# State-space layer: octets 0 and 1 driven between projection chunks 4 and 5, multiplier powers and later weights behind them on VectorE

## What is computed

```
u = h @ w_in                                   # 256 x 1024
lam_bar = exp(lam * dt)                        # 64 groups x 64 states, complex
b_bar = ((lam_bar - 1) / lam) * b
x[t] = lam_bar * x[t-1] + b_bar @ u[t]
y = real(c @ x) + d_skip * u
g = gelu(y)
val, gate = split(g @ w_glu)                   # 1024 -> 2 x 1024
mix = val * sigmoid(gate)
```

## Time and profile before

| what | us |
|---|---|
| median of 3 runs (802.72 to 804.08) | 803.85 |
| span of the profiled execution | 800.8 |
| state-space stage, to the end of y(3) | 124.5 |
| first scan starts on VectorE | 64.40 |
| GLU starts on TensorE | 98.22 |

### The profile page before, as it was taken

The page is one execution under the profiler, slowest core; times in us unless marked ns, Lnnn a source line. Parts: engine busy times, 40 slices in busy tenths (PEclk is TensorE's granted clock), DMA queues, the critical chain, the costliest instruction groups (busy, mean ns, idle before and its releaser), DMA issues.

```text
span 800.8 us, 16313 instructions
## 1 busy us (share of the span) xinstructions
PE 692.0 (86%) x6452; PEld 414.8 (52%) x6452; DVE 307.7 (38%) x853; ACT 243.7 (30%) x581; POOL 49.1 (6%) x48
## 2 busy tenths in 40 slices
PE   4999699999986686585899998899999999994995
PEld 4889445556544244244344444555555555652562
DVE  6968991144110010010241633736333443331334
ACT  6672802362110010110321314435223332231224
POOL 3695000000000000000000000000000000000000
PEclk9996899999998888988999999999999999998998
DMA  9530807977999999999992465038999942999981
GB/s 244 202 110 2 227 2 290 422 299 280 422 419 421 419 421 421 420 421 417 380 387 80 170 245 215 1 115 315 416 420 421 420 206 75 423 419 421 422 341 54
DMA packets 61071, 236.35 MB, mean 295 GB/s; under 512 B 21120, under 2 KB 21328, under 8 KB 36432
## 3 DMA queue, kind: packets, MB, share of 16 engines
q1 hardware_dynamic: 60112, 235.24, 74.2%
q10 hardware_dynamic: 896, 0.24, 0.1%
HBM read 234.42 MB, written 1.05 MB: 294 GB/s over the span
## 4 chain that ended last, share of the span: by engine, by line
PE 55%; SPq 16%; DMA 12%; DVE 10%; ACT 4%; issue 2%; DVEq 0%; ACTq 0%
SPq L425 13%; PE ps L1848 11%; PE ps L1939 10%; PE ps L1765 7%; PE ps L1903 6%; PE ps L1828 5%; DMA ring<-in_moe_w_up 4%; PE ps L1868 4%; DMA hT<-in_moe_w_up 3%; DMA ring<-in_moe_w_down 3%; SPq L423 3%; PE ps L2002 2%; PE ps L2013 2%; PE ps L1911 1%; PE ps L1636 1%
## 5 line engine op out<-in xcount | busy, mean ns | idle before, releaser
L1848 PE MATMUL ps<-ring,work 128*32 128x256 f32 x1504 | 124.3, 409 | 33.2 <-DMA ring<-in_moe_w_gate 11.7
L1848 PE MATMUL ps<-work 128*32 128x256 f32 x864 | 90.8, 409 | 23.9 <-DMA ring<-in_moe_w_up 7.8
L1848 PEld LDWEIGHTS ps<-ring,work 128*32 128x32 f32 x1504 | 70.3, 118 | 73.1 <-issue 51.8
L1381 DVE TENSOR_TENSOR work<-ps,work 128x256 f32<-128x256 f32 x21 | 12.9, 613 | 190.8 <-PE ps L1848 190.8
L1848 PEld LDWEIGHTS ps<-work 128*32 128x32 f32 x864 | 50.2, 118 | 54.4 <-issue 37.9
L1903 PE MATMUL ps<-ring,work 128*32 128x512 f32 x464 | 70.7, 611 | 6.2 <-issue 5.5
L1828 PE MATMUL ps<-work,xr 128*128 128x128 bf16 x736 | 66.5, 219 | 0.7 <-DVE work L1290 0.6
L1828 PE MATMUL ps<-work 128*128 128x128 bf16 x368 | 63.9, 219 | 0.0
L1828 PEld LDWEIGHTS ps<-work,xr 128*128 128x128 bf16 x736 | 57.6, 98 | 8.9 <-issue 3.3
L1939 PE MATMUL ps<-ring,hT 128*128 128x512 f32 x128 | 56.7, 595 | 1.2 <-ACT hT L632 1.2
L1765 PE MATMUL ps<-ring,work 128*128 128x512 f32 x128 | 55.7, 593 | 0.4 <-ACT work L749 0.4
(11 more groups left out here) (337 smaller groups left out, 1115.8 us busy)
## 6 DMA issues: line engine op xcount, KB each, us to landing
ring<-in_moe_w_down SPq DMA_DIRECT2D x22, 2048.0 KB, 24.4
ring<-in_moe_w_gate SPq DMA_DIRECT2D x21, 2048.0 KB, 20.0
ring<-in_moe_w_up SPq DMA_DIRECT2D x16, 2048.0 KB, 30.6
work<-in_moe_w_up SPq DMA_DIRECT2D x12, 2048.0 KB, 20.6
work<-in_moe_w_gate SPq DMA_DIRECT2D x9, 2048.0 KB, 29.0
work<-in_moe_w_down SPq DMA_DIRECT2D x8, 2048.0 KB, 23.7
ring<-in_ssm_w_glu SPq DMA_DIRECT2D x4, 2048.0 KB, 8.7
ring<-in_attn_w_qkv SPq DMA_DIRECT2D x4, 2048.0 KB, 27.9
```

The source lines that it names most:

```text
L1848: ins = mm(ps[s, 6 + j // 2, 0:256], xg[:, k, s], pairs[slots[e // 2]][e % 2][:, k, :], start=(k == 0), stop=(k == KD - 1))
```

## The change

Input weights are written by one instruction over both groups instead of two half-height ones, so W1 has each block twice; ScalarE keeps the transposed tile with a 0/1 scale per partition (new constants C_HALF), which takes the unwanted half to zero. So W1 needs no clearing and the power-0 copy comes from Bb itself. Mu and the skip product move behind weights(2) and weights(3). VectorE stacks half of octet 1's inputs, not octet 3's. Drive(0) and drive(1) both write banks 0 and 1 and come one after the other ahead of chunk 5; the first bank of each is copied to X by ScalarE, the second by VectorE. The scratch of the scan moves out of hT, which chunks 5 to 7 still read; the carries now wait for chunk 7 (u_done 8). ScalarE's BB copies, own(0) and own(1), VectorE's second skips, and glu(2) change places.

```
-        scanP, scanQ = (hT[:, 4 * n:4 * n + 4, :].rearrange("p k t -> p (k t)") for n in range(2))
+        scanP, scanQ = pre[:, 10240:10752], pre[:, 10752:11264]
+        V_AT = (0, 0, 0, 2)
...
-            clear(first_of[:, 0:2048], 2)
-            clear(second_of[:, 0:2048], 2)
...
+                for g in range(2):
+                    act.activation(W1T[o % 2][:, i, :, 64 * g:64 * g + 64], src[:, :, g, :], ACT.Copy,
+                                   scale=con[:, C_HALF + g:C_HALF + g + 1]).then_inc(w1T_ready, 1)
...
+            stack_by(0, range(6))
             first(0)
             first(1)
+            stack_by(0, range(6, 16))
             keep_w1T(0, 0)
-            stack_by(1, range(16))
+            stack_by(1, range(8, 12))
             keep_w1T(0, 1)
+            stack_by(1, range(12, 16))
+            keep_w1T(1, 0)
             first(2)
             keep_w1T(1, 1)
             first(3)
+            keep_x(0, (0,))
+            keep_x(1, (0,))
+            act.wait_ge(cleared, 3)
...
+            stack_by(2, range(4))
             keep_w1T(2, 0)
+            stack_by(2, range(4, 16))
             keep_w1T(2, 1)
+            stack_by(3, range(4))
             keep_w1T(3, 0)
+            stack_by(3, range(4, 16))
             keep_w1T(3, 1)
-            keep_x(2)
-            keep_x(3)
+            keep_x(2, (0, 1))
             own(0)
-            own(1)
+            keep_x(3, (0, 1))
...
             keep_g(1)
+            own(1)
...
-            link(dve.tensor_copy(mu[:, 0:2, 0, :], Pw[:, 0:2, 4, :]))
-            powers(mu, 1, 1, 0, 0)
-            powers(mu, 2, 2, 1, 0)
-            powers(mu, 4, 4, 3, 0)
-            link(TS(mu[:, 2, :, :], mu[:, 1, :, :], -1.0, None, ALU.mult))
             dve.sem_inc(pow_ready, 1)
...
-                    for g in range(2):
-                        h = slice(64 * g, 64 * g + 64)
-                        ins = TTo(W1[o % 2][h, i, :, 1:4, 16 * g:16 * g + 16], v3(t1)[h], v3(second_ps)[h],
-                                  ALU.add if i else ALU.subtract)
+                    link(TTo(W1[o % 2][:, i, :, 1:4, :].rearrange("p r j (g c) -> p r j g c", g=2), spread(v3(t1), 3, 2),
+                             spread(v3(second_ps), 3, 2), ALU.add if i else ALU.subtract))
+                    dve.sem_inc(w1_ready, 1)
...
             weights(0)
             weights(1)
+            dve.wait_ge(u_done, 4)
+            for n in range(8):
+                stack(dve.tensor_copy, 1, n).then_inc(u4_late, 1)
             weights(2)
+            link(dve.tensor_copy(mu[:, 0:2, 0, :], Pw[:, 0:2, 4, :]))
+            powers(mu, 1, 1, 0, 0)
+            powers(mu, 2, 2, 1, 0)
+            powers(mu, 4, 4, 3, 0)
+            link(TS(mu[:, 2, :, :], mu[:, 1, :, :], -1.0, None, ALU.mult))
             weights(3)
+            TTo(skip, spread(con[:, C_SKIP:C_SKIP + PC], 1, KD), spread(dcol, 2, PC), ALU.mult)
             for o in range(2):
-                for b in range(2):
-                    dve.wait_ge(v_done, 2 * o + b + 1)
-                    link(inputs_kept(dve.tensor_copy, o, b))
-                    dve.sem_inc(v_kept_x, 1)
+                dve.wait_ge(v_done, 2 * o + 2)
+                link(inputs_kept(dve.tensor_copy, o, 1))
+                dve.sem_inc(v_kept_x, 1)
...
                     skips(0)
+                    dve.wait_ge(u_done, 8)
                 carries(half)
+                carried(2 * half)
+                carried(2 * half + 1)
                 if half == 0:
                     skips(1)
...
+                    if r % 4 == 0:
+                        b = r // 4
+                        pe.wait_ge(u4_ready, (16 if b == 0 else 24, 24, 40, 56)[o])
+                        if o == 1 or (o == 0 and b == 1):
+                            pe.wait_ge(u4_late, 8)
+                        if o in (1, 2):
+                            pe.wait_ge(v_kept_x if b else v_kept_late, o)
...
+            inputs(1)
+            inputs(2)
             turn_w1(0, 0)
-            inputs(5)
+            inputs(3)
             turn_w1(0, 1)
-            inputs(6)
+            inputs(4, range(4))
             turn_w1(1, 0)
-            inputs(7)
+            inputs(4, range(4, KD))
             turn_w1(1, 1)
             drive(0)
+            drive(1)
+            inputs(5)
             turn_w1(2, 0)
+            inputs(6)
             turn_w1(2, 1)
-            drive(1)
+            taps(0)
+            taps(1)
+            inputs(7)
             turn_w1(3, 0)
             drive(2)
             turn_w1(3, 1)
-            taps(0)
-            taps(1)
             drive(3)
...
             glu(0, range(4))
+            glu(2, range(4))
             pe.wait_ge(f_ready, 32)
             glu(1, range(4))
-            glu(2, range(4))
```

More of the change, by code:

```diff
@@ L67 @@
 C_TURN = C_UPTO + 9 * 8
-C_N = C_TURN + 1
+C_HALF = C_TURN + 1
+C_N = C_HALF + 2
 def slot_plan():
@@ L660, in _ @@
                 act.copy(Cc[:, i, :, :].rearrange("p r c -> p (r c)"), ps[:, 4 + i, :]).then_inc(c_ready, 1)
-            act.wait_ge(cleared, 2)
+            act.wait_ge(cleared, 1)
             for i in range(2):
@@ L671, in stack_by @@
                     stack(act.copy, b, n).then_inc(u4_ready, 1)
[L673 to L677, removed]
-                for g in range(2):
-                    h = slice(64 * g, 64 * g + 64)
-                    act.copy(BB[i][h, :, 16 * g:16 * g + 16], Bb[h, i, :, :]).then_inc(block_b, 1)
             def first(o):
@@ L686, in first @@
                 if o == 0:
-                    act.wait_ge(block_b, 4)
+                    act.wait_ge(bbar_ready, 1)
                 for i in range(2):
-                    act.copy(W1[o % 2][:, i, :, 0, :], BB[i][:, OCT * o:OCT * o + OCT, :]).then_inc(w1_first, 1)
+                    act.copy(W1[o % 2][:, i, :, 0, :].rearrange("p r (g c) -> p r g c", g=2),
+                             spread(Bb[:, i, OCT * o:OCT * o + OCT, :], 2, 2)).then_inc(w1_first, 1)
             def keep_w1T(o, i):
@@ L695, in keep_w1T, with keep_x @@
                     act.wait_ge(v_done, 2 * o - 2)
-                for b in range(2):
[L697 to L702, removed]
+                src = ps[:, 4:6, :].rearrange("p b (r g c) -> p (b r) g c", g=2, c=64)
+                for g in range(2):
+                    act.activation(W1T[o % 2][:, i, :, 64 * g:64 * g + 64], src[:, :, g, :], ACT.Copy,
+                                   scale=con[:, C_HALF + g:C_HALF + g + 1]).then_inc(w1T_ready, 1)
+            def keep_x(o, bs):
+                for b in bs:
                     act.wait_ge(v_done, 2 * o + b + 1)
@@ L709, in own @@
                 if half == 0:
-                    act.wait_ge(cleared, 6)
+                    act.wait_ge(cleared, 4)
                 for j in range(SB):
@@ L715, in own @@
                         act.copy(dst[:, :, r, 32 * (3 - j):P], kps[:, :, 0:32 * (j + 1)]).then_inc(f_ready, 1)
+            act.wait_ge(normed, 2)
+            stack_by(0, range(6))
             first(0)
             first(1)
+            stack_by(0, range(6, 16))
             keep_w1T(0, 0)
-            stack_by(1, range(16))
+            stack_by(1, range(8, 12))
             keep_w1T(0, 1)
+            stack_by(1, range(12, 16))
+            keep_w1T(1, 0)
             first(2)
-            keep_w1T(1, 0)
-            stack_by(2, range(16))
             keep_w1T(1, 1)
             first(3)
-            stack_by(3, range(8, 16))
+            keep_x(0, (0,))
+            keep_x(1, (0,))
+            act.wait_ge(cleared, 3)
+            for i in range(2):
+                for g in range(2):
+                    h = slice(64 * g, 64 * g + 64)
+                    act.copy(BB[i][h, :, 16 * g:16 * g + 16], Bb[h, i, :, :]).then_inc(block_b, 1)
+            stack_by(2, range(4))
             keep_w1T(2, 0)
+            stack_by(2, range(4, 16))
             keep_w1T(2, 1)
+            stack_by(3, range(4))
             keep_w1T(3, 0)
+            stack_by(3, range(4, 16))
             keep_w1T(3, 1)
-            keep_x(2)
-            keep_x(3)
+            keep_x(2, (0, 1))
             own(0)
-            own(1)
+            keep_x(3, (0, 1))
             def gelu(o):
@@ L1169, in local_states @@
                 tmp = [v[:, 0:256].rearrange("p (i r h) -> p i r h", i=2, r=16) for v in (scanP, scanQ)]
-                if half:
-                    dve.wait_ge(v_kept_late, 4)
+                dve.wait_ge(v_kept_late, 6 if half else 2)
                 for l in range(1, SEG):
@@ L1625, in _, with inputs @@
             turn()
-            def inputs(c):
-                if c % 4 == 0:
+            def inputs(c, ks=range(KD)):
+                if c % 4 == 0 and ks[0] == 0:
                     pe.wait_ge(landed[c // 4], 16)
@@ L1632, in inputs @@
                     pe.wait_ge(bbar_ready, 1)
-                for k in range(KD):
+                for k in ks:
                     if c == 0 and k % 2 == 0:
@@ L1637, in inputs @@
```

(14 more changed lines are left out.)

37 lines of the change are left out of this document (8 added, 29 removed).

## The result

The changed kernel takes 812.16 us (median of 4 runs, 811.12 to 813.24) against 803.97 (4 runs, 802.72 to 804.27): ratio 1.0115, 95% interval 1.0102 to 1.0127. It is slower, by 8.2 us. The profiled execution took 811.12 with a span of 809.3.

The account below looks back on a forecast made before the run. The state-space stage of 125 us, with a fixed DMA-busy tail behind it, sets the time. The GLU starts at 106.0 against 98.22, taken as +8 on span 800.8: 808.8, plus 3.05 around it, 812; range 806 to 818.

Parts of the forecast that it names:

- VectorE's front: VectorE's input weights: paired writes at 0.95 for 1.13 us, 4.06 us an octet for 4.6, weights(2) ending at 42.4.
- the walk: The prediction's step-by-step timing of the engines through the state-space stage, putting the GLU's start at 106.0 against 98.22.
- TensorE up to drive(1): TensorE's chunks, transposes and drive(0): drive(0) runs to 43.8 us, the first bank of drive(1) to 45.6.
- The wait: Drive(1)'s second bank waits for VectorE's copy behind weights(2), mu, weights(3) and skip; TensorE stands 18.8 us from 45.6.
- Mu: Multiplier powers on VectorE, moved beside GpSimd's W2: held up by its SBUF reads, 15.4 us for 4.06, bounds 4.06 to 24.
- 11 rounds of 1.4: Mu's 8 linked groups wait out 11 GpSimd rounds, each 1.23 us of GpSimd and some 0.15 of VectorE: 15.4 us.
- From there: From mu's end to the GLU: second bank 3.5 us at low clock, scan at 68.9, own(0) last before y(0), +7.8.
- Rival (c): A second low-clock spell in octets 2 and 3: a drive at half speed, +3.5 us, 815.5; held for one in three.
- From span to time: Whole kernel: 3.05 us, the runs' median less the profiled span, added to the span of 808.8 to give 811.9.
- Left at zero: Effects given no cost: glu(2) ahead of glu(1), skips(1) behind the carried states (0.2 us), GLU weights loaded later.
- Rival (a): No hold-up of mu on VectorE: TensorE idles 6.4 us, about 800 us, or 796 without the low clock; chance 0.24.
- rival (b): One VectorE instruction a GpSimd round: mu 24 us, the GLU at 114.8, +16.6, 820 us; chance 0.12.

Follow-up runs that it names:

- 21 dummies: The changed kernel plus 21 matmuls of 512 columns, results unused, in TensorE's pause ahead of drive(1)'s second bank: 810.70 us, 1.0078 of the kernel before.

## Why the prediction was right

The sign, the size (812 for 812.16) and the mechanism came out, but that the size is so close is partly luck: terms missed in both directions.

1. *VectorE's front.* Writes of 768 elements took 0.95, as taken. An octet took 4.34 and not 4.06. Here the sum was wrong: 0.95 for 1.13, twice, makes 4.22 of 4.58. The rest is the wait of 0.15 behind the first write, which is now linked. The first instruction behind the powers came 0.9 later in this execution (24.00 for 23.13); weights(2) ended at 44.1, not 42.4. GpSimd began W2 at 25.80 and not at 23.5, since it also waits for ScalarE (the release in its row above, L661), which the walk had left out.
2. *TensorE up to drive(1)*: the first bank ended at 47.5 for 45.6. A low-clock stretch from 21 to 24.5, in this execution and not in the one before, took part of it: the execution with the later wait for chunk 7 hasn't got it, and the bank ends at 46.8 there, though weights(2) ends at 44.0 all the same.
3. *The wait* stood where it was put: VectorE's copy ended TensorE's pause, 15.85 us in place of 18.8. In two further executions of the changed order the pause was 17.84 (the changed kernel again) and 18.58 (the later wait).
4. *Mu*: 13.05 for 15.4, inside 11.2 to 24, in the execution profiled first. The changed kernel profiled again took 15.10 (44.61 to 59.71), with twelve instructions held and not ten. Three of its rows:

```profile
44.61 1.03 DVE L1139 COPY ring<-work 128x64 f32<-128x64 f32 x1
...
53.08 1.37 DVE L1091 TENSOR_TENSOR ring<-ring 128x128 f32<-128x128 f32 x1
...
58.37 1.30 DVE L1143 TENSOR_SCALAR ring<-ring 128x256 f32<-128x256 f32 x1
```

So the length isn't fixed: 13.05 and 13.3 with ten held, 15.10 to 15.33 with twelve (five executions), 16.37 with thirteen. In each that is about its own 4 us and some 0.9 for each hold. The prediction's 11 rounds of 1.4 are another split of nearly the same sum, and 15.4 fits most executions better than it fits the first. The count per round isn't fixed either: four of 32 elements passed in one, of 128 elements one or two. One reading of the earlier trace rows was wrong without harm: the GpSimd instructions there with which the two hold-ups ended are half-height subtractions (L557), not multiplies. They read SBUF too. That the hold-up is GpSimd's is shown by stopping GpSimd (13.05 to 4.05), that it costs what it costs by its place, by putting it behind the copies. The Trainium skill's rule (SBUF — State Buffer, Who interferes with whom) is what these runs show, down to its exception: one PSUM operand, no hold-up.
5. *From there.* The second bank at the low clock took 3.6, as taken (3.5), the scan began at 68.08 for 68.9. Here the walk named the wrong last step. Own(0) ended at 97.6 (for 99.0) and was not last:

```profile
90.56 7.03 ACT L709 COPY work<-ps 32x128 f32<-32x128 f32 x16
```

Rival (c) came true: drive(3) took 7.09 at the low clock and the taps behind it 3.38, and y(0) started at 99.9 behind them, 2.3 later than own(0) would have let it. By the walk it was 99.0 behind own(0). So in this execution a short mu and the spell of (c), held for one in three and left out of the sum, cancelled: that the size came out so closely is luck. In the two further executions mu was as long as taken, own(0) ended at 100.8 and 100.1, and the spell (93.5 to 103.7, 92.4 to 102.6) put y(0) at 102.6 and 102.3. It was there with 21 dummies too (89.6 to 99.9), and every profiled execution of this study, of the kernel before as well, has at least one such spell between 72 and 106 us. It should have been in the sum. No run takes it away, so its price is read from the chain alone.
6. *From span to time.* The 3.05 taken as what lies around the span isn't that. It is 1.8 here (811.12 less 809.3) and 1.8 in the other runs; the rest is how far that one execution lies below the median. Span against span the forecast was 808.8 for 809.3.
7. *Left at zero*: the GLU's loads, own(1) and glu(2) did no harm, the GLU block taking 20.87 in one piece as before. The wait ahead of the carries (1.65 us) did none either, as the run with it moved shows.

Rival (a) fell with mu's rows, rival (b) with the count. The price list of (a), about 800, has no run with just its condition. Two come near: 801.5 with mu in front, and 802.72 with mu unheld at its new place. In both GpSimd held the scan instead, which (a) hadn't counted.

## What to carry to other kernels

Before a chain of small instructions is moved "into idle time" on VectorE, look at what GpSimd does there: with both operands in SBUF, half of them and more were held for most of a microsecond, and a block of 4 us became 13 to 16. If it must overlap, give each two-operand instruction one operand in PSUM, and put the chain behind, not ahead of, whatever another engine waits for. A wait that stops TensorE can cost twice, by the pause and by the low clock behind it: here some 3 us on top of a pause of 16 to 18.

## What the runs showed of the hardware beyond that

A plain copy and a tensor_scalar from SBUF to SBUF were held as well (0.94 for 0.20, 1.23 for 0.29, in the rows of the run with the copies ahead). Short instructions that follow each other without a link can slip through together, up to four of 32 elements (44.50 to 45.78 in the changed kernel's rows). And TensorE can be busy without a break and stay at the low level: drive(3), 64 columns to a load of 128, ran all its 7.1 us at 0.50 in the changed kernel, and so did the 13.6 us of drives and transposes in the earlier trace rows; what brought the clock back is not settled here.
